# One core, a decoder layer in float32: values copied by bank, a shorter chain before the last scaling, and the weights of a compressed piece made one step later

## The chip, the cores and the metric

The kernel is one program on one core of a Trainium2 chip. The metric is the device time of one execution in microseconds (us), lower is better. Engines are named as in the profile: PE (TensorE, matmuls), PEld (its weight loads), DVE (VectorE), ACT (ScalarE), POOL (GpSimd), SP (the queue that issues most transfers).

## What is computed

The reference is one decoder layer over 256 tokens of width 2048. Two attention groups run side by side on one normed input, latent attention (MLA, 8 heads) and sparse attention (NSA, 16 heads), and their outputs are joined, projected, and followed by a squared-ReLU MLP and a last RMS norm. Cut to what the change touches:

```python
# values of MLA
kv = (rmsnorm(c_kv, kv_norm_w) @ w_ukv).reshape(B, T, MLA_HEADS, MLA_NOPE + MLA_V)
k_nope, v = kv[..., :MLA_NOPE], kv[..., MLA_NOPE:]
# NSA: keys and values compressed over blocks of 32 tokens, stride 16
blk = t[:, tok_idx] + pos[None, None, :, None, :]
k_cmp = gelu(blk @ w1) @ w2
# one head's three branches; the compressed one has 15 keys
p_c = masked_softmax(s, dist >= 0);  o_c = p_c @ v_cmp
return g0 * o_c + g1 * o_s + g2 * o_w
# end of the layer
return rmsnorm(h + square(relu(n @ w_up)) @ w_down, final_norm_w)
```

With 256 tokens every block is selected, so the selected and the window branch both see all earlier tokens.

## The kernel before, in words

Every engine has its own instruction list, written out by hand, and they meet through semaphores alone. Float32 products are made from two parts: ACT copies a weight chunk to a high part (`w_hi`, L587, L594), DVE subtracts to get the low part (`w_lo`, L885), and PE multiplies high by high, high by low and low by high. Weight chunks are numbered in the order of use.

The attention stage is a table of steps, `STEPS`: eight MLA steps, then for each pair of NSA heads five steps, `slc` and `win` of the first head, `slc` and `win` of the second, and `cmp` for both. Each engine runs `slot(i)` for i = 0, 1, 2, ..., with products of the output projection (`("q", ...)`, L1387 to L1391) and weight splits between the slots, in the order of the list `PLAN`. `LAG` is 4. In slot i

- PE makes the scores of step i (L1617, L1618 for `slc`, which also serves the `win` step after it), transposes the finished weights of step i-4 (L1635; L1630 for a `cmp` step), and multiplies those of step i-5 by the values (L1662, L1663; L1649 for `cmp`);
- DVE adds the bias to the scores of step i and takes the extreme (`masked`, L1034), and scales the exponentials of step i-2 (`weights`, L1061 to L1065; those of `slc` and `win` together);
- ACT copies PE's transposes out (L694; L692 for `cmp`) and then makes the exponentials of step i-1 (L717, L718).

The scores of the compressed branch are made for four heads at a time, in four pieces. `PIECES` maps slots 12, 22, 32 and 42 to pieces 0 to 3. In such a slot PE makes the piece's scores (L1584) and DVE takes them in (`piece_in`, L1024 to L1028); ACT makes its exponentials one slot later (L724). DVE's `piece_weights` (L1041 to L1047 and one L885 on `pcs`) turns them into weights and raises `pc_ok`, for which PE waits before it transposes the `cmp` step at L1630, four slots after the piece's scores:

```python
if kind == "cmp":
    pe.wait_ge(pc_ok, h // 4 + 1)
```

Two other places matter. The value product of MLA (chunk 20) leaves tokens 0 to 127 in PSUM banks 4 and 5; DVE copies both to `v_sb` (L1011) and raises `v_out`. The first layer of the compression (chunks 21, 23 for keys in bank 4, chunks 25, 27 for values in bank 5; L1708, L1709) waits for that before its first chunk. At the end, `root(t, ...)` (L1315) makes one over the root mean square of the tokens of half t: ACT sums the last squares (L836, `fsq`) and takes a square root (L848, `sqrt_ok`), DVE meanwhile prepares minus half the mean square (L1318, L1319) for one Newton step on the reciprocal (L1321 to L1323). `link` makes the next DVE instruction wait for the one that it wraps.

Of the kernel before, what the change touches and what calls it, by code (L numbers as in the profile page):

```python
# [61 lines left out]
def split_slot(c):  # L62
    return (c + 1) % SPLIT
# [79 lines left out]
def build(nc, a, out):  # L143
    with ExitStack() as ctx:
# [729 lines left out]
        def _(dve):  # L874
            chain = [0]

            def link(ins):
                chain[0] += 1
                ins.then_inc(dve_c, 1)
                dve.wait_ge(dve_c, chain[0])  # L880
# [127 lines left out]
            low(blk[:, :, :, 32:32 + 2 * NC].rearrange("p y k n -> p (y k) n"), blkf[:, :, :, :].rearrange("p y k n -> p (y k) n"),  # L1008
                blk[:, :, :, 0:2 * NC].rearrange("p y k n -> p (y k) n")).then_inc(blk_ok, 1)
            dve.wait_ge(w_used, UKV_V + 1)  # L1010
            dve.tensor_copy(v_sb[:, 0, :], flat[:, 2048:3072]).then_inc(v_out, 1)  # L1011

            STEP_OF = {n: i for i, n in SOFT.items()}
            vfull = h1a[:, 0, :].rearrange("p (g d) -> p g d", g=NG)
# [52 lines left out]
            def slot(i):  # L1067
                kind, u, h, branch = STEPS[i] if i < len(STEPS) else ("cmp", 0, 0, 0)
                if kind == "mla":
                    n = SOFT[i]  # L1070
                    dve.wait_ge(score_t, n + 1)
                    if n == 0:
                        dve.wait_ge(q_lo, 4)
                    masked(n, [ps[:, 4 + i % 2, 0:P], ps[:, 4 + i % 2, P:SEEN]], mask)
                elif kind == "slc":
                    n = SOFT[i]
                    dve.wait_ge(score_t, n + 2)
                    dve.wait_ge(bias_ok, h + 1)
                    for b in range(2):
                        masked(n + b, [ps[:, 4, P * b:P * b + P], ps[:, 5, T * b:T * b + T]], (bias_even, bias_odd)[h % 2])  # L1080
                if i in PIECES:
                    piece_in(PIECES[i], 5)
                if i == SUM0:
                    mean_square(0, rm[:, :])
                if 0 <= i - 2 < len(STEPS):
                    weights(STEPS[i - 2][0], STEPS[i - 2][2], SOFT.get(i - 2))
                if i - 2 in PIECES:
                    piece_weights(PIECES[i - 2])
                j = i - LAG - 1
                if j >= 0 and LASTSTEP[STEPS[j][1]] == j:  # L1090
                    u = STEPS[j][1]
                    dve.wait_ge(y_hi, u + 1)
                    low(yT[:, u, 1, :], ysb[:, u % 2, :], yT[:, u, 0, :], wcols[:, PRM["y"] + u:PRM["y"] + u + 1]).then_inc(y_lo, 1)
# [218 lines left out]
                dve.scalar_tensor_tensor(out=o, in0=flat[:, b0 + c0:b0 + c1], scalar=r1[:, t:t + 1], in1=o,  # L1312
                                         op0=ALU.mult, op1=ALU.add).then_inc(last_in, 1)

            def root(t, part, rest, done):  # L1315

                y, w, minus, mean = rc[:, t:t + 1], rc[:, 2 + t:3 + t], root_w[:, t:t + 1], root_w[:, 2 + t:3 + t]
                link(dve.scalar_tensor_tensor(out=mean, in0=part, scalar=1.0 / D, in1=rest, op0=ALU.mult, op1=ALU.add))  # L1318
                link(dve.tensor_scalar(minus, mean, -0.5, None, ALU.mult))  # L1319
                dve.wait_ge(sqrt_ok, t + 1)  # L1320
                link(dve.reciprocal(y, rm[:, t:t + 1]))  # L1321
                link(dve.scalar_tensor_tensor(out=w, in0=y, scalar=minus, in1=y, op0=ALU.mult, op1=ALU.mult))
                dve.scalar_tensor_tensor(out=y, in0=w, scalar=1.5, in1=y, op0=ALU.add, op1=ALU.mult).then_inc(done, 1)  # L1323
# [11 lines left out]
            dve.wait_ge(fsq, 2)  # L1335
            dve.tensor_scalar(ssq[:, 12:13], ssq[:, 12:13], 1.0 / D, EPS, ALU.mult, ALU.add).then_inc(rest_ok, 1)
            dve.wait_ge(rest_ok, 1)
            dve.wait_ge(fsq, 3)
            root(0, ssq[:, 13:14], ssq[:, 12:13], root0)
            dve.wait_ge(last_t, 1)  # L1340
            last_add(1, 1024, 1536)
            dve.wait_ge(root0, 1)
# [13 lines left out]
            dve.scalar_tensor_tensor(out=ssq[:, 14:15], in0=ssq[:, 10:11], scalar=1.0 / D, in1=ssq[:, 14:15],  # L1356
                                     op0=ALU.mult, op1=ALU.add).then_inc(rest_ok, 1)
            dve.wait_ge(rest_ok, 2)
            dve.wait_ge(fsq, 6)
            root(1, ssq[:, 11:12], ssq[:, 14:15], root1)  # L1360
            dve.wait_ge(root1, 1)
            last_norm(1, 1024, 1280)
            last_norm(1, 1280, D)
# [3 lines left out]
        def _(pe):  # L1367
# [320 lines left out]
            for kind, i in PLAN:  # L1688
                if kind in "wq" and (i in A_IN if kind == "w" else i[0] in A_IN):
                    c, quarter = (i, None) if kind == "w" else i  # L1690
                    j = A_IN.index(c)
                    if j in (0, 2):
                        pe.wait_ge(kv_out, 3 + j // 2)
                    if j == 4:
                        pe.wait_ge(qs_lo, 2)
                    q_products(c, quarter)
                elif kind == "w":
                    if i == CMP[0]:
                        pe.wait_ge(blk_ok, 1)
                        pe.wait_ge(v_out, 1)  # L1700
                    y, half, s = CMP.index(i) // 2, CMP.index(i) % 2, split_slot(i)
                    o = ps[0:64, 4 + y, 0:CMP_HID]
                    for b in range(8):
                        k = 8 * half + b
                        w = slice(CMP_HID * b, CMP_HID * b + CMP_HID)
                        if b % 4 == 0:
                            split_done(i, b == 0)
                        pe.matmul(o, blk[:, y, k, :], w_hi[:, s, w], start=k == 0, stop=False)  # L1708
                        m = pe.matmul(o, blk[:, y, k, :], w_lo[:, s, w], start=False, stop=k == 15)  # L1709
                        if b == 3:  # L1710
                            m.then_inc(w_half, 1)
                    m.then_inc(w_used, 1)
                elif kind == "q":
                    c, quarter = i
                    n, j, part = (c - WO_M) // 4, (c - WO_M) % 4, (c - WO_M) // 8

                    def free(t, n=n):
                        if n:
                            pe.wait_ge(dve_free, 2 * n - 1 + t)
                        else:  # L1720
                            pe.wait_ge(q_in, 2 * t + 2)
                    if n % 2 == 0 and quarter % TT == 0:
                        pe.wait_ge(y_lo, 8 * part + 2 * j + 1 + quarter // TT)
                    stream(c, of_y, 8 * part + 2 * j, LOW, j == 0, j == 3, free, quarter)
                elif kind == "s":
                    slot(i)
                elif kind == "keys":
                    pe.wait_ge(kn_out, i + 1)
                    turn_kd(2 + i, i)
                elif i == "rotary":  # L1730
                    pe.wait_ge(kn_out, 4)
                    pe.wait_ge(qpr_ok, 2)
                    for c in range(4):
                        for t in range(TT):
                            o = T * (c % 2) + P * t
                            m = pe.transpose(ps[:, 2 + c // 2, o:o + P], qpr[:, t, P * c:P * c + P], ident[:, :])
                        if c % 2:
                            m.then_inc(qp_t, 1)
                elif i == "rotary_k":
                    pe.wait_ge(v_rest, 1)  # L1740
                    pe.wait_ge(kpe_ok, 2)
                    for t in range(TT):
                        m = pe.transpose(ps[:, 6, P * t:P * t + P], kpe[:, t, :], ident[:, :])
                    m.then_inc(qp_t, 1)
                elif i == "turn":
                    pe.wait_ge(g_ok, 1)
                    pe.wait_ge(kp_lo, 1)
                    for y in range(2):
                        for k in range(2):
                            o = 2 * NC * (2 * y + k)  # L1750
                            m = pe.transpose(ps[:, 6, o:o + 2 * NC], h1a[:, y, P * k:P * k + P], ident[0:2 * NC, 0:2 * NC])
                    m.then_inc(g_t, 1)
                elif i == "project":
                    pe.wait_ge(g_turned, 1)
                    pe.wait_ge(w2_in, 48)
                    for k in range(2):
                        pe.matmul(ps[:, 7, 0:2 * NC], w2k[:, k, :, :].rearrange("p c d -> p (c d)"), h1T[:, k, :],
                                  start=k == 0, stop=k == 1)
                    for g in range(NG):
                        for k in range(2):  # L1760
                            m = pe.matmul(ps[0:2 * NC, 7, 64 + DK * g:64 + DK * g + DK],
                                          h1V[:, 2 * k + g, :, :].rearrange("p e n -> p (e n)"), w2v[:, k, :],
                                          start=k == 0, stop=k == 1)
                    m.then_inc(k_t, 1)
                elif i == "rows":
                    pe.wait_ge(rbc_ok, 2)
                    for t in range(TT):
                        m = pe.transpose(ps[:, 7, P * t:P * t + P], rtmp[:, 0, P * t:P * t + P], ident[:, :])
                    m.then_inc(rr_t, 1)
                elif i == "norm_n":  # L1770
                    sum_over_features(1)
# [123 lines left out]
```

## Time and profile before

| what | value |
|---|---|
| device time, median of 3 runs | 1051.85 us (1051.05 to 1051.92) |
| the profiled execution, device time | 1051.07 us |
| the profiled execution, span | 1049.3 us |
| PE busy | 1036.7 us |
| DVE busy | 637.0 us |
| ACT busy | 503.4 us |
| mean granted clock of PE | 0.997 |

The device time of the profiled execution is 1.8 us over its span, which reaches from the first to the last instruction on the core. Times in rows are counted from the span's start. Busy times of PE are modelled, so single gaps are read from the starts of its instructions. The attention slots lie between about 150 and 305 us, the MLP's loop between about 330 and 1020 us.

### The profile page before, as it was taken

What the parts mean: (1) busy time and instruction counts of PE and PEld (TensorE: products, weight loads), DVE (VectorE), ACT (ScalarE), POOL (GpSimd) and SP (SyncE); (2) the same over time, 40 slices, a digit from 0 to 9 for tenths busy, and PEclk for the clock granted to TensorE, in tenths of its full rate; (3) what the DMA queues carried; (4) which work ended last, traced back from release to release, by engine and by line L of the source; (5) the groups of instructions that cost most, each with busy time, mean ns of one, the idle gap of its engine ahead of it and who ended that gap; (6) DMA issues with size and microseconds to landing.
All of it is one profiled execution on the core that took longest, in us unless ns stands there. A gap on an engine that the chain in (4) does not pass through costs nothing.

```text
span 1049.3 us, 14380 instructions
## 1 busy us (share of the span) xinstructions
PE 1036.7 (99%) x5631; PEld 896.3 (85%) x5631; DVE 637.0 (61%) x761; ACT 503.4 (48%) x630; POOL 92.5 (9%) x152
## 2 busy tenths in 40 slices
PE   8999999999999999999999999999999999999996
PEld 7889999888888888888888888888888888888885
DVE  4655976988856564565456556545554555655666
ACT  5645855977754543344334443334434433433434
POOL 2135100633200100000000000000000000000002
PEclk9999999999999999999999999999999999999998
DMA  9576672343346566566556655665566565656662
GB/s 330 181 209 199 210 242 81 142 141 97 105 130 192 162 196 188 182 195 199 185 180 195 198 180 187 195 198 183 181 197 196 182 185 196 196 177 189 198 201 80
DMA packets 89137, 190.42 MB, mean 181 GB/s; under 512 B 8758, under 2 KB 29964, under 8 KB 88716
## 3 DMA queue, kind: packets, MB, share of 16 engines
q1 hardware_dynamic: 88668, 189.41, 57.3%
q10 hardware_dynamic: 432, 0.52, 0.2%
q8 instruction: 23, 0.38, 0.1%
q14 instruction: 14, 0.11, 0.0%
HBM read 187.82 MB, written 2.10 MB: 181 GB/s over the span
## 4 chain that ended last, share of the span: by engine, by line
PE 95%; DVE 2%; ACT 1%; issue 0%; DMA 0%; DVEq 0%; ACTq 0%
PE ps L1805 23%; PE ps L1387 15%; PE ps L1388 15%; PE ps L1391 15%; PE ps L1808 12%; PE ps L1678 1%; PE ps L1679 1%; PE ps L1682 1%; PE ps L1662 1%; PE ps L1635 1%; PE ps L1460 1%; PE ps L1663 1%; PE ps L1513 1%; PE ps L1512 1%; PE ps L1511 1%
## 5 line engine op out<-in xcount | busy, mean ns | idle before, releaser
L885 DVE TENSOR_TENSOR w_lo<-raw,w_hi 128x2048 fp32r<-128x2048 f32 (+4 forms) x198 | 402.4, 2034 | 355.3 <-ACT w_hi L594 289.3
L594 ACT ACTIVATE w_hi<-raw 128x2048 fp32r<-128x2048 f32 x119 | 228.1, 1917 | 399.3 <-PE ps L1391 200.7
L1805 PE MATMUL ps<-xT,w_hi 128*128 128x512 f32 x1024 | 279.4, 394 | 0.0
L1805 PEld LDWEIGHTS ps<-xT,w_hi 128*128 128x128 f32 x1024 | 176.1, 189 | 24.2
L1808 PEld LDWEIGHTS ps<-xT,w_lo 128*128 128x128 f32 x1024 | 157.2, 189 | 21.7
L1388 PE MATMUL ps<-w_lo,hidT 128*128 128x512 f32 x448 | 174.6, 390 | 0.0
L1387 PE MATMUL ps<-w_hi,hidT 128*128 128x512 f32 x448 | 174.6, 390 | 0.0
L1808 PE MATMUL ps<-xT,w_lo 128*128 128x256 f32 x1024 | 162.9, 281 | 0.0
L1391 PE MATMUL ps<-w_hi,hidT 128*128 128x512 f32 x448 | 138.2, 390 | 0.0
L587 ACT ACTIVATE w_hi<-raw 128x1024 fp32r<-128x1024 f32 (+3 forms) x75 | 104.2, 1392 | 67.9 <-PE ps L1391 40.9
L1391 PEld LDWEIGHTS ps<-w_hi,hidT 128*128 128x128 f32 x448 | 84.1, 188 | 17.6
L1388 PEld LDWEIGHTS ps<-w_lo,hidT 128*128 128x128 f32 x448 | 84.2, 188 | 17.2
L1387 PEld LDWEIGHTS ps<-w_hi,hidT 128*128 128x128 f32 x448 | 84.1, 188 | 17.1
L556 POOL TENSOR_TENSOR h_sb<-h_sb,fw 128x1024 f32<-128x1024 f32 x2 | 6.2, 3114 | 676.5 <-ACT sink L836 676.5
L1387 PE MATMUL ps<-w_hi,yT 128*128 128x512 f32 x128 | 54.0, 422 | 0.3 <-DVE h_sb L1121 0.3
L1388 PE MATMUL ps<-w_lo,yT 128*128 128x512 f32 x128 | 50.2, 392 | 0.0
L1387 PE MATMUL ps<-w_hi,xT 128*128 128x512 f32 x112 | 39.7, 355 | 0.0
L1391 PE MATMUL ps<-w_hi,yT 128*128 128x512 f32 x128 | 39.7, 392 | 0.0
L1388 PE MATMUL ps<-w_lo,xT 128*128 128x512 f32 x112 | 37.9, 349 | 0.0
L1678 PE MATMUL ps<-xT,w_hi 128*128 128x256 f32 x128 | 36.7, 286 | 0.0
L1679 PE MATMUL ps<-xT,w_hi 128*128 128x256 f32 x128 | 36.2, 283 | 0.0
L1682 PE MATMUL ps<-xT,w_lo 128*128 128x256 f32 x128 | 36.2, 283 | 0.0
(339 smaller groups left out, 1267.5 us busy)
## 6 DMA issues: line engine op xcount, KB each, us to landing
raw<-in_w_up SPq DMA_DIRECT2D x64, 1024.0 KB, 5.3
raw<-in_w_down SPq DMA_DIRECT2D x64, 1024.0 KB, 5.5
raw<-in_w_o SPq DMA_DIRECT2D x16, 1024.0 KB, 5.5
raw<-in_w_in SPq DMA_DIRECT2D x8, 1024.0 KB, 5.3
raw<-in_w_in SPq DMA_DIRECT2D x8, 816.0 KB, 4.5
raw<-in_w_in SPq DMA_DIRECT2D x6, 832.0 KB, 9.0
raw<-in_mla_w_uq SPq DMA_DIRECT2D x12, 256.0 KB, 4.6
raw<-in_mla_w_ukv SPq DMA_DIRECT2D x4, 512.0 KB, 4.9
```

The source lines that it names most:

```text
L587: act.activation(w_hi[:, split_slot(c), w0:w1], raw[:, raw_slot(c), w0:w1], ACT.Copy)\
L594: act.activation(w_hi[:, j % SPLIT, :], raw[:, j % RAW, :], ACT.Copy).then_inc(hi_done, 1)
L885: return dve.tensor_tensor(dst, src, high.bitcast(F32), ALU.subtract)
L1387: pe.matmul(o, stationary(0, b, t), w_hi[:, slot, w], start=first, stop=False)
L1388: pe.matmul(o, stationary(0, b, t), w_lo[:, slot, w], start=False, stop=False)
L1391: m = pe.matmul(o, stationary(1, b, t), w_hi[:, slot, b * width + n0:b * width + n1], start=False, stop=last)
L1460: m = pe.matmul(flat[:, LOW[t] + n0:LOW[t] + n1], of_x(part, 2 * c + b, t), w_part[:, split_slot(c), CW * b + n0:CW * b + n1], start=c == ...
L1678: pe.matmul(o, w_hi[:, s, w], xT[:, 0, k, :], start=k == 0 and f == 0, stop=False)
L1679: m = pe.matmul(o, w_hi[:, s, w], xT[:, 1, k, :], start=False, stop=False)
L1682: m = pe.matmul(o, w_lo[:, s, w], xT[:, 0, k, :], start=False, stop=k == KT - 1 and f == 1)
L1805: pe.matmul(both, w_hi[:, slot, 512 * b + P * f:512 * b + P * f + P], xT[:, :, k0 + b, :], start=start and b == 0, stop=False)
L1808: m = pe.matmul(ps[:, b0 + f, 0:T], w_lo[:, slot, 512 * b + P * f:512 * b + P * f + P], xT[:, 0, k0 + b, :], start=False, stop=stop and b ...
```

## The change

It has three edits. The copy of the MLA values from banks 4 and 5 becomes two copies of one bank each, and each of the compression's products waits only for its own bank. In the last chain, DVE's two small operations before the reciprocal are put another way, so that one of them needs only what is there before the last sum of squares. And DVE calls `piece_weights` in slot i for the piece of slot i-3, where it was i-2. PE's list of instructions stays as it is.

```diff
             dve.wait_ge(w_used, UKV_V + 1)
-            dve.tensor_copy(v_sb[:, 0, :], flat[:, 2048:3072]).then_inc(v_out, 1)
+            for n in range(2):
+                dve.tensor_copy(v_sb[:, 0, 512 * n:512 * n + 512], bank(4 + n)).then_inc(v_out, 1)
...
                 if 0 <= i - 2 < len(STEPS):
                     weights(STEPS[i - 2][0], STEPS[i - 2][2], SOFT.get(i - 2))
-                if i - 2 in PIECES:
-                    piece_weights(PIECES[i - 2])
+                if i - 3 in PIECES:
+                    piece_weights(PIECES[i - 3])
...
-            def root(t, part, rest, done):
+            def root(t, part, rest, before, done):
 
-                y, w, minus, mean = rc[:, t:t + 1], rc[:, 2 + t:3 + t], root_w[:, t:t + 1], root_w[:, 2 + t:3 + t]
-                link(dve.scalar_tensor_tensor(out=mean, in0=part, scalar=1.0 / D, in1=rest, op0=ALU.mult, op1=ALU.add))
-                link(dve.tensor_scalar(minus, mean, -0.5, None, ALU.mult))
+                y, w, minus, half = rc[:, t:t + 1], rc[:, 2 + t:3 + t], root_w[:, t:t + 1], root_w[:, 2 + t:3 + t]
+                link(dve.tensor_scalar(half, rest, -0.5, None, ALU.mult))
+                dve.wait_ge(fsq, before)
+                link(dve.scalar_tensor_tensor(out=minus, in0=part, scalar=-0.5 / D, in1=half, op0=ALU.mult, op1=ALU.add))
                 dve.wait_ge(sqrt_ok, t + 1)
                 link(dve.reciprocal(y, rm[:, t:t + 1]))
...
             dve.wait_ge(rest_ok, 1)
-            dve.wait_ge(fsq, 3)
-            root(0, ssq[:, 13:14], ssq[:, 12:13], root0)
+            root(0, ssq[:, 13:14], ssq[:, 12:13], 3, root0)
...
             dve.wait_ge(rest_ok, 2)
-            dve.wait_ge(fsq, 6)
-            root(1, ssq[:, 11:12], ssq[:, 14:15], root1)
+            root(1, ssq[:, 11:12], ssq[:, 14:15], 6, root1)
...
                     if i == CMP[0]:
                         pe.wait_ge(blk_ok, 1)
-                        pe.wait_ge(v_out, 1)
                     y, half, s = CMP.index(i) // 2, CMP.index(i) % 2, split_slot(i)
+                    pe.wait_ge(v_out, y + 1)
```

The third edit moves instructions on DVE. This is DVE's list before, from slot 34 (the third piece, scored in slot 32) into slot 35: a weight split, the piece's six instructions, and then the first of slot 35's biased scores. The rest of those scores and then the scaling of step 33 (L1061 to L1065) follow.

```order
L885 TENSOR_TENSOR w_lo<-raw,w_hi 128x1024
L1041 TENSOR_REDUCE cden<-pc 128x8
L1042 RECIPROCAL cden<-cden 128x8
L1043 TENSOR_TENSOR cden<-cden,cgate 128x8
L1044 TENSOR_TENSOR pc<-pc,cden 128x120
L1047 CAST pcs<-pc 128x4x2x30
L885 TENSOR_TENSOR pcs<-pc,pcs 128x4x30
L1034 ISA prob,nmax<-ps,bias_odd 128x128
L1034 ISA nmax 128x1
```

This is the end of slot 35 on DVE in the changed kernel (its lines are numbered one higher from L1012 on): the last of the biased scores, the scaling of step 33, and now the piece's six instructions.

```order
L1035 ISA nmax 128x1
L1062 RECIPROCAL scl<-den 128x4
L1063 TENSOR_TENSOR scl<-scl,gates 128x4
L1065 TENSOR_TENSOR prob<-prob,scl 128x2x128
L1066 TENSOR_TENSOR prob<-prob,scl 128x2x256
L1042 TENSOR_REDUCE cden<-pc 128x8
L1043 RECIPROCAL cden<-cden 128x8
L1044 TENSOR_TENSOR cden<-cden,cgate 128x8
L1045 TENSOR_TENSOR pc<-pc,cden 128x120
L1048 CAST pcs<-pc 128x4x2x30
L885 TENSOR_TENSOR pcs<-pc,pcs 128x4x30
L885 TENSOR_TENSOR w_lo<-raw,w_hi 128x1024
```

The six instructions moved from ahead of slot 35's eight score instructions and four scaling instructions to behind them. At the other three pieces the same six move past the same twelve; at piece 0 also past the two low parts of the queries (`q2b`), and at pieces 1 and 3 past a weight split.

This is DVE's second `root` before, from the sum that it starts with to the reciprocal.

```order
L1356 SCALAR_TENSOR_TENSOR ssq<-ssq 128x1
L1318 SCALAR_TENSOR_TENSOR root_w<-ssq 128x1
L1319 TENSOR_SCALAR root_w<-root_w 128x1
L1321 RECIPROCAL rc<-rm 128x1
L1322 SCALAR_TENSOR_TENSOR rc<-rc,root_w 128x1
```

And this is the same place in the changed kernel.

```order
L1357 SCALAR_TENSOR_TENSOR ssq<-ssq 128x1
L1319 TENSOR_SCALAR root_w<-ssq 128x1
L1321 SCALAR_TENSOR_TENSOR root_w<-ssq,root_w 128x1
L1323 RECIPROCAL rc<-rm 128x1
L1324 SCALAR_TENSOR_TENSOR rc<-rc,root_w 128x1
```

The count is the same; the wait for the last sum of squares stood ahead of the first of the two `root_w` operations and now stands between them.

## Rows read from the trace of the kernel before

**Rows 1.** The page: busy time of each engine

```profile
PE 1036.7 (99%) x5631; PEld 896.3 (85%) x5631; DVE 637.0 (61%) x761; ACT 503.4 (48%) x630; POOL 92.5 (9%) x152
```

**Rows 2.** Stretches: PE, PEld, DVE, ACT, POOL busy (count), clock, DMA share, GB/s

```profile
320.00:1020.00 700.00, 700.00 (x3565) 596.41 (x3564) 391.88 (x240) 282.15 (x194) 3.52 (x1) 1.00 0.61 190
```

**Rows 3.** PE's waits after 100 us: us in total, times, longest

```profile
PE ps L1635 <- DVE prob L1065: 0.6, 1, 0.6
```

**Rows 4.** Timeline of DVE around piece 2: start, us, instruction

```profile
259.29 0.27 DVE L1041 TENSOR_REDUCE cden<-pc 128x8 f32<-128x120 f32 x1
...
260.67 0.28 DVE L885 TENSOR_TENSOR pcs<-pc,pcs 128x120 fp32r<-128x120 f32 x1
260.87 0.28 DVE L1034 CUSTOM_DVE_ANT_0 prob<-ps,bias_odd 128x128 f32<-128x128 f32 x1
...
261.98 0.17 DVE L1061 RECIPROCAL scl<-den 128x4 f32<-128x4 f32 x1
...
263.33 1.22 DVE L885 TENSOR_TENSOR w_lo<-raw,w_hi 128x1024 fp32r<-128x1024 f32 x1
```

**Rows 5.** Timeline of PE, slots 35 and 36

```profile
259.88 0.40 PE L1618 MATMUL ps<-k2l,q2b 128*128 128x512 f32 x1
...
262.49 0.38 PE L1630 MATMUL ps<-ident,pcs 128*96 128x128 f32 x2
```

**Rows 6.** Timeline around piece 0, and the next `q2b` pair

```profile
206.07 1.27 ACT L771 ACTIVATE q2b<-qfb 64x512 fp32r<-64x512 f32 x2
...
208.87 0.38 PE L1630 MATMUL ps<-ident,pcs 128*96 128x128 f32 x2
...
219.13 1.27 ACT L771 ACTIVATE q2b<-qfb 64x512 fp32r<-64x512 f32 x2
...
221.26 0.29 DVE L1034 CUSTOM_DVE_ANT_0 prob<-ps,bias_odd 128x128 f32<-128x128 f32 x1
```

**Rows 7.** Timeline of DVE and PE around piece 1

```profile
233.20 0.26 DVE L1041 TENSOR_REDUCE cden<-pc 128x8 f32<-128x120 f32 x1
...
234.77 1.22 DVE L885 TENSOR_TENSOR w_lo<-raw,w_hi 128x1024 fp32r<-128x1024 f32 x1
...
237.77 0.69 DVE L1065 TENSOR_TENSOR prob<-prob,scl 128x512 f32<-128x512 f32 x1
...
235.58 0.38 PE L1630 MATMUL ps<-ident,pcs 128*96 128x128 f32 x2
...
237.40 0.62 PE L1391 MATMUL ps<-w_hi,yT 128*128 128x512 f32 x2
238.60 0.52 PE L1635 MATMUL ps<-ident,prob 128*128 128x128 f32 x3 [0.58 <-DVE prob L1065]
```

**Rows 8.** Timeline of DVE and PE around the values' copy

```profile
115.05 1.22 DVE L1011 COPY v_sb<-ps 128x1024 f32<-128x1024 f32 x1
...
117.31 0.69 DVE L885 TENSOR_TENSOR k2l<-ps,k2h 128x512 fp32r<-128x512 f32 x1
...
115.13 1.04 PE L1736 MATMUL ps<-ident,qpr 128*128 128x128 f32 x8
116.37 0.30 PE L1708 MATMUL ps<-w_hi,blk 128*64 128x256 f32 x1 [0.20 <-issue]
...
118.29 0.28 PE L1678 MATMUL ps<-xT,w_hi 128*128 128x256 f32 x1
```

**Rows 9.** Timeline of the last chain, tokens 128 to 255

```profile
1042.93 0.29 ACT L848 ACTIVATE rm<-ssq 128x1 f32<-128x1 f32 x1
...
1043.38 0.16 DVE L1321 RECIPROCAL rc<-rm 128x1 f32<-128x1 f32 x1
```

**Rows 10.** PE's last matmul, and stretches behind it (columns as in rows 2)

```profile
1041.07 0.28 PE L1858 MATMUL ps<-w_end,hidZ 128*128 128x256 f32 x1
...
1043.00:1044.00 1.00, 0.00 (x0) 0.00 (x0) 0.85 (x5) 0.22 (x1) 0.00 (x0) 1.00 1.03 422
1044.00:1044.50 0.50, 0.00 (x0) 0.00 (x0) 0.47 (x2) 0.47 (x1) 0.00 (x0) 0.50 0.43 164
```

## Prediction, made before the result was known

> **What bounds the kernel now.** I read the page's first part first: PE is busy for 1036.7 of 1049.3 us and no other engine comes near [rows 1]. Then the stretches: in the MLP's 700 us PE is busy for all 700 at full clock [rows 2]. So a microsecond that PE loses in the attention stage isn't won back later. It moves everything behind it, and the end. Then PE's own waits after 100 us: the longest is 0.6 us, for the scaled probabilities of DVE at L1065 [rows 3]. The kernel is bound by PE's stream, with DVE close behind it in the attention slots. There the question for any edit on DVE is when a result is ready and when PE comes for it, so I went to the timelines of both engines at the three places that the change touches.
>
> **The piece's weights, one slot later.** PE's list doesn't move: it still comes for `pc_ok` in the fourth slot after the piece's scores. What moves is DVE's part, from ahead of the next slot's twelve instructions to behind them. Those twelve can't be done before PE has made that slot's scores. This gives a floor that can be worked out from four durations, all at piece 2:
>
> - The six instructions of the piece run from 259.29 to 260.67 + 0.28 = 260.95, so 1.66 us [rows 4].
> - Slot 35's biased scores run from 260.87 to 261.98, 1.11 us, and the scaling from there to 263.33, 1.35 us [rows 4].
> - PE's scores of slot 35 end at 259.88 + 0.40 = 260.28, and PE comes for the piece at 262.49 [rows 5]. That is 2.21 us.
> - A hand-over from DVE to PE takes 0.14 us: L1065 ends at 237.77 + 0.69 = 238.46 and PE's L1635, which waited for it, starts at 238.60 [rows 7].
>
> Before, the piece was ready 1.54 us ahead of PE (262.49 - 260.95). Now DVE needs 1.11 + 1.35 + 1.66 + 0.14 = 4.26 us after the scores are there, and PE leaves it 2.21. PE stalls for 2.05 us; with a hand-over of up to 0.14 from PE to DVE as well, 2.19. I take **2.1**. DVE's earlier start doesn't help, since the scores hold it: without the piece it would be free at 259.29 and the scores end at 260.28. The exponentials that the scaling needs are no later than before. Piece 3 has the same distance between the same two PE rows and the same twelve instructions; the weight split that is moved past there too finds room ahead of the scores. So the rows of piece 2 stand for both: 2 x 2.1 = **4.2**.
>
> At piece 1 DVE runs behind PE, with no idle time in these rows. Between 233.20 and 238.46 it does the piece, a weight split (234.77), the biased scores, and the scaling that ends with L1065 [rows 7]. The same instructions in another order end at the same time, 238.46, now with the piece's last one. PE comes for it at 235.58 and would go on at 238.60: a stall of **3.0**. In return the wait for L1065 at 238.60 goes, 0.58 by its row, since the scaling is now 1.6 us earlier and PE is later: **-0.6**. The floor here is the 2.1 of piece 2, were DVE not behind.
>
> At piece 0 the `q2b` pair stands behind the piece too. It can't start early, since it waits for ACT's pair of copies, started at 206.07. At the next such place DVE idles for ACT, and slot 20's biased scores start 221.26 - 219.13 = 2.13 us after ACT's pair [rows 6]. So here they start at 206.07 + 2.13 = 208.20. Then 1.11 + 1.35 + 1.66 + 0.14 gives 212.46, and PE comes at 208.87 [rows 6]: a stall of **3.6**. That second `q2b` place also matters because DVE there falls in step with ACT, and ACT with PE's transposes. The lead over PE that DVE wins in the first stall is gone before piece 1.
>
> Together 3.6 + 3.0 - 0.6 + 4.2 = 10.2 us. ACT is held in each stall too, as its list has the copy of PE's transpose (L692) ahead of the exponentials. They then come as much later as PE does, and the next use of each is two slots off, so I charge nothing for that. If that cover were gone, another wait of up to the same length would follow.
>
> **The clock.** The last matmul ends at 1041.07 + 0.28 = 1041.35. The granted clock is still 1.00 (2.4 GHz) in the stretch to 1044.00 and 0.50 (1.2 GHz) from there [rows 10]. So it held for 2.65 us of idleness and then fell. Stalls of 2.1 us are shorter than that, those of 3.0 and 3.6 longer. Were it to fall, no row shows how long it stays down once PE works again. I bound that by the time that it took to fall: 2.65 us at half speed lose 1.3 us, so 0 to 1.3 for each of the two long stalls. In the sum I take 0, as one observation with nothing behind it, no matmul at all, is not a stall inside a dense stream.
> The Trainium skill, "TensorE: Matmul & The Clock Gate", Part 1, has the low clock as the default that activity lifts, and its section on oscillation has a stream that waits for operands falling back at its breaks. The trace agrees that the clock falls after idleness. By that rule alone the sum would be up to 2.7 us higher, and by the row's 2.65 us it stays where it is for two of the four stalls at least.
>
> **The values by bank.** L1708 starts at 116.37, 0.10 after the copy of both banks ends at 115.05 + 1.22 = 116.27 [rows 8]. PE's eight transposes before it end at 116.17 by their row, so the wait costs at least 0.20, as the row says, and at most 0.4, if L1708 could follow the transposes at their own pace (1.04 us for eight with the overlap of the last, so some 0.11 each: 115.13 + 8 x 0.11 = 116.0). The first half copy is done by some 0.7 after 115.05 (a 128x512 on DVE takes 0.69), so this wait goes. What is late next is `k2l`: PE needs it for its next product at 118.29, and it ends at 117.31 + 0.69 = 118.00 at the earliest, a little later with the second copy's overhead [rows 8]. With the hand-over of 0.14 the product can't start before 118.14. Gain 0 to 0.4; I take **-0.1**.
>
> **The last chain.** The square root ends at 1042.93 + 0.29 = 1043.22 and the reciprocal starts at 1043.38, behind the two small operations [rows 9]. One of them now lies in DVE's wait for the sum of squares. The reciprocal still needs the root, so at most 0.16 is to be had, and nothing at the least; **-0.1**. The first `root` has the root as its last input already and lies beside PE's work: 0.
>
> **Sum.** 10.2 - 0.1 - 0.1 = +10.0 us. The profiled execution took 1051.07 us (span 1049.3), which gives 1061.1. It lies 0.8 below the median of the runs shown, 1051.85, from which it would be 1061.9. I forecast between them, **1061.4 us**.
>
> **Rivals.**
>
> - *Four stalls, clock held* (my forecast), 0.50: 1061.4, its own range 1060.3 to 1062.4.
> - *The clock falls in one or both of the long stalls*, 0.28: +1.3 or +2.7, so 1062.7 to 1064.1. For it speaks that 3.0 and 3.6 exceed 2.65 us; against it, that PE is dense on both sides. The page named above is this rule.
> - *DVE gets ahead for good*, 0.15. If the lead after the first stall lasts, or ACT's pair at piece 0 comes sooner, every stall shrinks toward the floor: 4 x 2.1 - 0.6 - 0.2 = +7.6, 1059.0. Against it speaks DVE's idle time for ACT ahead of 221.26.
> - *Faster*, 0.04. One mechanism, the wait at L1635: if the piece were ready when PE comes, only the gains would be left, 0.6 + 0.1 + 0.1, so 1050.6. It decides at 2.21 us between scores and transposes: DVE would have to do 4.26 us of work in them, or PE to come 2.1 us later than its rows say. Nothing in the rows shows such slack.
> - *No change by measure*, 0.03: the stalls are taken up by waits that PE has anyway. Rows 3 name the longest as 0.6, so there is too little to take up. That the edit doesn't reach the instructions is excluded by their order.
>
> A measurement tells about 0.2% here, 2.1 us. Slower by more: 0.50 + 0.28 + 0.15 = 0.93. Within: 0.03. Faster: 0.04. The range runs from the third case's 1059.0, a little below, to the second's 1064.1, a little above: 1058.8 to 1064.2.
>
> **What would show it.** In the changed profile PE idles ahead of L1630 four times, for about 3.6, 3.0, 2.1 and 2.1 us, released by DVE's L885 on `pcs`, and ACT's wait for L692 grows by the same. PE's wait at L1635 for L1065 is gone. L1708 starts some 0.3 us earlier after its transposes, L1678 about 0.1. The reciprocal of the second `root` starts less than 0.16 after the square root's end. The granted clock between 205 and 245 us tells the second case. I am wrong if DVE does the piece before slot i's scores in time, or if PE's L1630 starts within 0.5 us of where its stream reaches it.

## The result and the profile after

The changed kernel takes 1067.19 us (median of 4 runs, 1065.64 to 1067.36), the kernel before 1051.82. The ratio is 1.0145, 95% interval 1.0132 to 1.0157: 15.4 us slower. The direction was forecast, the size was not: 1067.2 lies above the range's 1064.2.

The profiled execution took 1067.03 us with a span of 1065.2, 15.9 more than before. The first two lines of its page answer to [rows 1]: PE has the same 5631 instructions and 6.5 us more of busy time, which no added work explains.

```profile
span 1065.2 us, 14384 instructions
...
PE 1043.2 (98%) x5631; PEld 900.4 (85%) x5631; DVE 636.8 (60%) x762; ACT 503.5 (47%) x630; POOL 93.3 (9%) x152
```

PE's waits in the attention slots (in total, times, longest). The wait of [rows 3] is gone, and the one that was forecast is there four times:

```profile
PE ps L1630 <- DVE pcs L885: 10.1, 4, 3.4
PE ps L1387 <- DVE h_sb L1122: 0.3, 1, 0.3
```

The four places on PE's timeline: the last product before the wait, then the first transpose of the piece, with PE's idle time in brackets.

```profile
208.38 0.62 PE L1391 MATMUL ps<-w_hi,yT 128*128 128x512 f32 x2
212.40 0.63 PE L1630 MATMUL ps<-ident,pcs 128*96 128x128 f32 x2 [3.40 <-DVE pcs L885]
...
241.34 0.61 PE L1391 MATMUL ps<-w_hi,yT 128*128 128x512 f32 x2
244.80 0.40 PE L1630 MATMUL ps<-ident,pcs 128*96 128x128 f32 x2 [2.85 <-DVE pcs L885]
...
272.06 0.63 PE L1391 MATMUL ps<-w_hi,yT 128*128 128x512 f32 x2
274.64 0.40 PE L1630 MATMUL ps<-ident,pcs 128*96 128x128 f32 x2 [1.94 <-DVE pcs L885]
...
300.32 0.63 PE L1391 MATMUL ps<-w_hi,yT 128*128 128x512 f32 x2
302.89 0.40 PE L1630 MATMUL ps<-ident,pcs 128*96 128x128 f32 x2 [1.94 <-DVE pcs L885]
```

From the first of L1391's two products to L1630 a stream without a wait takes about 0.46 us (235.12 to 235.58 in the kernel before). The stalls are the rest: 4.02 - 0.46 = 3.56, then 3.00, 2.12 and 2.11 us, each as forecast. The times in brackets are up to 0.2 us shorter; below, "idle" means the bracket and "stall" the loss by the starts. DVE at the third of them, as the floor in the prediction had it: the biased scores wait for PE's scores, then 1.12 us of them, 1.35 of scaling, and 1.67 for the piece, which ends 0.15 before L1630 starts.

```profile
270.35 0.29 DVE L1035 CUSTOM_DVE_ANT_0 prob<-ps,bias_odd 128x128 f32<-128x128 f32 x1 [0.94 <-PE ps L1618]
...
271.47 0.17 DVE L1062 RECIPROCAL scl<-den 128x4 f32<-128x4 f32 x1
...
272.82 0.27 DVE L1042 TENSOR_REDUCE cden<-pc 128x8 f32<-128x120 f32 x1
...
274.21 0.28 DVE L885 TENSOR_TENSOR pcs<-pc,pcs 128x120 fp32r<-128x120 f32 x1
```

So the stalls are 10.8 us. The wait that went was worth 0.74 by the starts (L1391 at 237.40 to L1635 at 238.60 is 1.20 in the kernel before, where 0.46 is the pace), which leaves 10.05. The span grew by 15.9. The rest is in the stretches (length, busy time of PE, PEld, DVE, ACT, POOL, then granted clock, DMA share, GB/s):

```profile
208.00:211.20 3.20, 1.00 (x5) 0.47 (x3) 3.03 (x16) 0.91 (x1) 0.00 (x0) 1.00 0.97 324
211.40:218.00 6.60, 5.60 (x20) 4.86 (x20) 2.30 (x7) 3.07 (x10) 0.00 (x0) 0.50 0.43 171
218.20:244.80 26.60, 23.75 (x133) 19.81 (x131) 22.40 (x69) 16.77 (x46) 9.88 (x19) 1.00 0.25 80
245.40:248.60 3.20, 3.20 (x11) 2.42 (x10) 1.52 (x5) 1.96 (x9) 0.00 (x0) 0.50 0.52 127
248.80:303.40 54.60, 50.72 (x284) 42.84 (x283) 40.40 (x129) 35.23 (x100) 13.65 (x11) 1.00 0.27 88
303.60:306.80 3.20, 3.20 (x10) 2.42 (x10) 1.53 (x5) 1.85 (x9) 0.00 (x0) 0.50 0.51 146
```

The granted clock is at 0.50 (1.2 GHz) in three stretches, each of which begins in a stall or within 0.6 us of its end, and lasts about 6.8, 3.4 and 3.4 us. I call such a change from 1.00 to 0.50 a fall. What that does to the matmuls is seen in the spacing of the products behind the fourth stall, 0.43 us in place of 0.24:

```profile
304.56 0.63 PE L1388 MATMUL ps<-w_lo,yT 128*128 128x512 f32 x1
304.99 0.63 PE L1387 MATMUL ps<-w_hi,yT 128*128 128x512 f32 x1
...
307.00 0.36 PE L1649 MATMUL ps<-probR,vcmp 96*128 96x256 f32 x1
307.20 0.40 PE L1387 MATMUL ps<-w_hi,yT 128*128 128x512 f32 x1
307.44 0.40 PE L1388 MATMUL ps<-w_lo,yT 128*128 128x512 f32 x1
```

From L1630 to L1649 it is 307.00 - 302.89 = 4.11 us here and 291.11 - 288.61 = 2.50 in the kernel before: 1.6 us for one stretch of 3.4. Behind the second stall it is 4.11 too (3.30 in the kernel before, with the wait for L1065 in it, and 2.52 in an execution of the changed kernel whose clock held there), behind the first 5.51 where it was 2.90, so 1.6 and 2.6. Together 5.8 us, and 10.05 + 5.8 = 15.9.

### The profile page after: what moved, and what is told of

It reads as the page before. It is cut to its first block, busy times and chain, and to the rows that moved or that the text cites. A ratio compares the mean times of both kernels' runs of the same rounds, so it can differ in the third digit from the quotient of the medians.

```text
span 1065.2 us, 14384 instructions
## 1 busy us (share of the span) xinstructions
PE 1043.2 (98%) x5631; PEld 900.4 (85%) x5631; DVE 636.8 (60%) x762; ACT 503.5 (47%) x630; POOL 93.3 (9%) x152
## 4 chain that ended last, share of the span: by engine, by line
PE 93%; DVE 4%; ACT 2%; issue 1%; DMA 0%; DVEq 0%; ACTq 0%
PE ps L1805 22%; PE ps L1387 15%; PE ps L1388 15%; PE ps L1391 15%; PE ps L1808 11%; PE ps L1678 1%; PE ps L1679 1%; PE ps L1682 1%; PE ps L1662 1%; PE ps L1460 1%; PE ps L1635 1%; DVE prob L1035 1%; PE ps L1663 1%; PE ps L1513 1%; PE ps L1511 1%
## 5 line engine op out<-in xcount | busy, mean ns | idle before, releaser
L1805 PE MATMUL ps<-xT,w_hi 128*128 128x512 f32 x1024 | 279.3, 394 | 0.0
L1805 PEld LDWEIGHTS ps<-xT,w_hi 128*128 128x128 f32 x1024 | 176.0, 189 | 24.3
L1388 PE MATMUL ps<-w_lo,hidT 128*128 128x512 f32 x448 | 174.4, 389 | 0.0
L1391 PE MATMUL ps<-w_hi,hidT 128*128 128x512 f32 x448 | 138.1, 389 | 0.0
L1391 PEld LDWEIGHTS ps<-w_hi,hidT 128*128 128x128 f32 x448 | 84.1, 188 | 17.6
L1388 PEld LDWEIGHTS ps<-w_lo,hidT 128*128 128x128 f32 x448 | 84.1, 188 | 17.2
L1387 PE MATMUL ps<-w_hi,yT 128*128 128x512 f32 x128 | 55.6, 434 | 0.3 <-DVE h_sb L1122 0.3
L1388 PE MATMUL ps<-w_lo,yT 128*128 128x512 f32 x128 | 51.6, 403 | 0.0
L1391 PE MATMUL ps<-w_hi,yT 128*128 128x512 f32 x128 | 41.0, 403 | 0.0
L1388 PE MATMUL ps<-w_lo,xT 128*128 128x512 f32 x112 | 37.9, 348 | 0.0
L1678 PE MATMUL ps<-xT,w_hi 128*128 128x256 f32 x128 | 36.7, 287 | 0.1
```

The costliest lines, as they stand in the source:

```text
L1387: pe.matmul(o, stationary(0, b, t), w_hi[:, slot, w], start=first, stop=False)
L1388: pe.matmul(o, stationary(0, b, t), w_lo[:, slot, w], start=False, stop=False)
L1391: m = pe.matmul(o, stationary(1, b, t), w_hi[:, slot, b * width + n0:b * width + n1], start=False, stop=last)
L1678: pe.matmul(o, w_hi[:, s, w], xT[:, 0, k, :], start=k == 0 and f == 0, stop=False)
L1805: pe.matmul(both, w_hi[:, slot, 512 * b + P * f:512 * b + P * f + P], xT[:, :, k0 + b, :], start=start and b == 0, stop=False)
```

## The experiments

One measure is used for all. Executions differ in how long their first 85 us take: PE's first product of chunk 16 (L1523) starts between 84.87 and 86.62 us in the profiled ones, and between 85.11 and 86.03 in the four of the changed kernel. So beside the times I give the **way**: from that product to the MLP's first matmul (L1805), in the profiled execution. It is 331.66 - 85.11 = 246.55 us before and 347.56 - 85.11 = 262.45 in the changed kernel: +15.9, the whole difference of the spans. Four executions of one kernel further down have ways from 248.60 to 248.66, so a few hundredths of a microsecond are noise. The way ends before the last chain, of which it says nothing.

### Which edit it is

The first kernel puts the pieces' weights back, the second makes that edit alone.

```diff
-                if i - 3 in PIECES:
-                    piece_weights(PIECES[i - 3])
+                if i - 2 in PIECES:
+                    piece_weights(PIECES[i - 2])
```

> The changed kernel with the piece's weights made in slot i-2 again, so that only the copy by bank and the shorter chain are left. Theory: the two edits are worth 0.1 us together, PE never waits at L1630 and the clock stays at 1.00, so -0.1 us against the kernel before (1051.7). Rival: one of the two small edits carries part of the loss of 15.4 us; then this is over 1053.

> The kernel before with only the piece's weights moved to slot i-3. Theory: all of the loss is here, +15.5 us (between +13.8 and +17, by how many of the stalls end with the clock at 1.2 GHz). Rival: the edits work on each other, and this alone loses clearly less.

Measured: 1051.62 us with the pieces back, ratio 1.0003 (0.9993 to 1.0012), way 246.50. With the pieces alone 1067.66 us, ratio 1.0153 (1.0136 to 1.0170), way 262.48. All of the loss is in this edit. The copy by bank is worth 0.05 us of way at most, no more than the noise of the way, and neither small edit shows in the times.

### The stalls without the clock

The rival to "stalls and a lower clock" was that a stall brings further waits behind it. Here PE is kept at work during the stalls, on transposes whose output nothing uses.

```diff
+                        if j in PIECES:
+                            for _ in range((30, 24, 17, 17)[PIECES[j]]):
+                                pe.transpose(ps[:, 6, SEEN:SEEN + P], ident[:, :], ident[:, :])
                         pe.wait_ge(pc_ok, h // 4 + 1)
```

> The changed kernel, in which PE makes 30, 24, 17 and 17 transposes of the identity into an unused part of bank 6 ahead of its four waits for the piece's weights (some 0.11 us each, so 3.2, 2.6, 1.8 and 1.8 us, less than the stalls of 3.6, 3.0, 2.1 and 2.1). Nothing else is changed and their output is not used. Theory (stalls of 10.1 us in all, and 5.8 us from the clock falling during them): the clock stays at 1.00 and the time is +10.0 us against the kernel before. Rival (the 5.8 us are knock-on waits or contention after a stall, and the clock's level follows something else): still +15.4 us.

Measured: 1060.83 us, ratio 1.0091 (1.0074 to 1.0108), +9.3 us. All four runs lie between 1060.65 and 1060.91. The way is 256.34, +9.8. The clock stays at 1.00, and PE comes to the first piece's transposes 127.2 us after the product at 85 us (212.06 - 84.87), where it was 127.3 with an idle stall (212.40 - 85.11):

```profile
205.00:335.00 130.00, 129.48 (x732) 109.89 (x731) 91.83 (x251) 79.87 (x207) 25.98 (x32) 1.00 0.38 124
```

```profile
208.56 3.44 PE L1630 MATMUL ps<-ident 128*128 128x128 f32 x30
212.06 0.42 PE L1633 MATMUL ps<-ident,pcs 128*96 128x128 f32 x2
```

PE has more work, and the way is 6.1 us shorter than the changed kernel's (by the times 15.4 - 9.3 = 6.1 too). This parts the loss: 9.8 us of way are the stalls, and 6.1 went with the idleness. Most of the 6.1 is the clock. The four stalls are 0.06 to 0.10 us shorter each than the idle ones (3.96 for 4.02 from L1391 to the piece's transposes at the first), 0.3 together, so 5.8 is left for the clock, which is what the rows above gave.

### Half of each stall filled

The same with 15, 12, 8 and 8 transposes.

> As the kernel with the stalls filled, with half as many transposes (15, 12, 8 and 8), so that PE still idles for about 2.0, 1.7, 1.2 and 1.2 us in each stall. The stalls' 10 us stay in any case. If the clock falls by the length of idle time alone and 1.9 us is near the least that does it (it fell at one of the two stalls of that length in the changed kernel), at most one fall is left: +10 to +11.6 us. If any stall of this kind can bring it down, two or three falls: +13 to +15.

Measured: 1060.79 us (1060.48 to 1061.42), ratio 1.0087 (1.0070 to 1.0104), way 256.23. PE still idles for 5.1 us in four waits (1.68, 1.43, 0.98 and 0.98), and the clock is at 1.00 throughout the attention slots. The first outcome came, with no fall at all. The mean granted clock was 0.998 in all four runs, and so it was in the four with the stalls filled:

```profile
209.42 1.80 PE L1630 MATMUL ps<-ident 128*128 128x128 f32 x15
...
212.90 0.42 PE L1633 MATMUL ps<-ident,pcs 128*96 128x128 f32 x2 [1.68 <-DVE pcs L885]
```

### One piece late at a time

The edit for piece 0; those for pieces 2 and 3 differ only in the numbers.

```diff
-                if i - 3 in PIECES:
-                    piece_weights(PIECES[i - 3])
+                for back, those in ((2, (1, 2, 3)), (3, (0,))):
+                    if PIECES.get(i - back) in those:
+                        piece_weights(PIECES[i - back])
```

> The changed kernel with only piece 0 one slot later, the others in slot i-2. Theory: one stall of 3.6 us and 2.6 us of PE work at 1.2 GHz behind it (1.6 if the low clock lasts as it did at pieces 1 and 3), so +6.1 or +5.1 us; the stall at piece 1 for L1065 is as before. Rival: the lead that DVE wins stays, and the wait for L1065 at piece 1 shrinks, so 0.7 less.

> The changed kernel with only piece 2 one slot later. Theory: a stall of 2.1 us at PE and nothing else, +2.0 us; if the clock falls in it as it did at piece 3 of the changed kernel, +3.6 us. Rival: a stall of 2.1 us is taken up elsewhere, under +1.

> The changed kernel with only piece 3 one slot later. Same stall of 2.1 us: +2.0 us with the clock held, +3.6 us with a fall. If falls come by chance with the moment, runs of this kernel and of the one with piece 2 late lie on two levels 1.6 us apart; if the place decides, piece 3 is always +3.6 and piece 2 always +2.0.

Measured with piece 0 late: 1057.18 us, ratio 1.0057 (1.0040 to 1.0073), way 251.59, +5.0. PE's idle time at the piece is 3.43 us, the clock is at 0.50 for 3.4 us from 0.2 us before its end, and the wait for L1065's result at piece 1 is 0.6 us as before. So DVE's lead is lost by then, and the third rival of the prediction is out.

With piece 2 late: 1054.67 us, ratio 1.0028 (1.0017 to 1.0038), way 248.66, +2.1, clock held. With piece 3 late: 1054.68 us, ratio 1.0030 (1.0020 to 1.0040), way 248.60, +2.05, clock held. The ways and the clock are those of the profiled executions. A stall of 2.1 us goes to the end in full.

Each median is a microsecond more than the way of the profiled execution tells. The mean granted clock, which is measured in every run, says why for the most part. A fall of 3.4 us takes 1.7 us of clock off some 1054, 0.0016 of the mean. It was 0.997 to 0.999 in every run of the kernel before, and 0.996 in the two profiled executions with one fall of 3.4 us (piece 0 late, and the piece between, below). The nine runs of piece 3 are these:

| mean granted clock | times, us |
|---|---|
| 0.998 or 0.999 | 1053.23, 1053.40 (profiled), 1053.61, 1054.15, 1054.68 |
| 0.996 | 1055.83, 1056.03, 1056.03, 1056.12 |

So four of the nine had a fall, at the same stall in the same kernel. Of the eight runs of piece 2, four were at 0.996 too (1054.68 to 1055.17), one at 0.997, which tells neither, and three at 0.998 or 0.999 (1054.03 to 1054.65); there the two groups lie less than 1.6 us apart. The runs without a fall have medians of 1053.61 and 1054.31, +1.95 and +2.65 against the kernel before.

> The same kernel as with only piece 3 late, profiled again. Its nine times lay near 1053.4 and near 1056. If falls come by the moment and not by the place, the profile shows one stall of 1.9 to 2.0 us in every execution and the clock at 0.50 behind it in some of them, with 1.6 us more from L1630 to the MLP's first matmul in these.

> The same kernel once more, same expectation: the stall always, the fall in some executions, 1.6 us apart.

> The same kernel once more, same expectation: the stall always, the fall in some executions, 1.6 us apart.

These gave 1053.45, 1054.10 and 1053.52 us, ways of 248.66, 248.65 and 248.63, and no fall in any. The mean clock was 0.998 in each. The expectation of falls in some was not met by these three; it had been met by the nine before them.

### The same kernel again

> The changed kernel unchanged, profiled again. The four stalls at L1630 are the same as before in length to 0.1 us (3.6, 3.0, 2.1, 2.1). If the falls of the clock come by the moment, their number and length differ between executions, and the way from the first product of chunk 17 (85 us) to the MLP's first matmul differs with them: 246.5 + 10.0 us, plus 1.6 us for each fall of one period (3.4 us) at 1.2 GHz. If the place decides: three falls, at pieces 0, 1 and 3, and 262.4 us each time.

> The changed kernel once more, same expectation as for the first repeat: stalls the same, 246.5 + 10.0 us of way plus 1.6 us per 3.4 us at 1.2 GHz; by the moment, the number differs; by the place, 262.4 us again.

> The changed kernel once more, same expectation as for the first repeat: stalls the same, 246.5 + 10.0 us of way plus 1.6 us per 3.4 us at 1.2 GHz; by the moment, the number differs; by the place, 262.4 us again.

(The product at 85 us is the first of chunk 16.) The times were 1064.35, 1066.78 and 1067.91 us, the ways 259.46, 262.21 and 262.42. PE's wait at L1630 is 10.1, 10.1 and 10.2 us. The stretches at 0.50, in the first,

```profile
212.20:215.40 3.20, 2.68 (x9) 2.33 (x10) 1.47 (x3) 2.01 (x9) 0.00 (x0) 0.50 0.80 321
...
300.80:304.00 3.20, 3.20 (x10) 2.46 (x9) 1.53 (x5) 2.00 (x9) 0.00 (x0) 0.50 0.49 120
```

and in the second:

```profile
211.00:217.60 6.60, 5.18 (x17) 4.44 (x18) 2.29 (x7) 3.07 (x10) 0.00 (x0) 0.50 0.48 182
245.20:248.40 3.20, 3.20 (x10) 2.55 (x9) 1.52 (x5) 2.01 (x9) 0.00 (x0) 0.50 0.50 124
275.80:279.00 3.20, 3.20 (x11) 2.59 (x10) 1.37 (x4) 2.75 (x9) 0.00 (x0) 0.50 0.00 0
```

The first has falls at pieces 0 and 3, the second at 0, 1 and 2, the third at 0, 1 and 3, with 6.8 us at piece 1 and not at piece 0. The same stalls bring different falls: it is the moment, not the place. Nor has PE to be idle when the clock changes. At piece 2 of the second, L1630 starts at 274.46 and the stretch at 0.50 only 1.3 us later:

```profile
274.46 0.40 PE L1630 MATMUL ps<-ident,pcs 128*96 128x128 f32 x2 [1.94 <-DVE pcs L885]
...
275.83 0.63 PE L1387 MATMUL ps<-w_hi,yT 128*128 128x512 f32 x1
276.26 0.63 PE L1388 MATMUL ps<-w_lo,yT 128*128 128x512 f32 x1
```
In the first, with two stretches of 3.4 us, the way is 3.1 us longer than with the stalls filled, about 1.6 for each, as expected.

### Where DVE's order is the hold-up, and where it isn't

Two more tested the floor's arithmetic and the wait of [rows 3]. In one, slot i makes the weights of slot i-3's piece between its biased scores and its scaling, ahead of the scaling and not behind it; in the other the pieces are back and one weight split of DVE moves behind slot 25.

```diff
+                if i - 3 in PIECES:
+                    piece_weights(PIECES[i - 3])
                 if 0 <= i - 2 < len(STEPS):
                     weights(STEPS[i - 2][0], STEPS[i - 2][2], SOFT.get(i - 2))
-                if i - 3 in PIECES:
-                    piece_weights(PIECES[i - 3])
```

```diff
+LATE_SPLIT = NMLA + 17
...
-        behind = [i for i in split if i[0] == "lo" and _s in PIECES]
+        behind = [i for i in split if i[0] == "lo" and (_s in PIECES or _s == LATE_SPLIT)]
```

> The changed kernel with the piece's weights in slot i-3 between the biased scores and the scaling, 1.35 us sooner than behind the scaling. By the floor's arithmetic the stalls become 2.2, 1.7, 0.75 and 0.75 us, less 0.7 for the wait at L1065: +4.6 us with the clock held, +6.2 with one fall at piece 0. Rival (the hold-up isn't DVE's order after the scores): stalls as in the changed kernel, +10 or more.

> The piece's weights in slot i-2, the two small edits kept, and the weight split that stands ahead of slot 25 on DVE (first half of chunk 38) put behind that slot, 1.1 us of work out of the way of the scaling of step 23, for which PE waited 0.7 us at L1635. Theory: that wait goes, -0.8 us against the kernel before. Rival: the half split is then late for PE, or the wait moves to the next scaling: 0 or more.

Measured with the piece between: 1057.73 us, ratio 1.0051 (1.0034 to 1.0068), way 252.74, +6.2. PE idles for 2.05, 1.49, 0.59 and 0.59 us at the four pieces, 1.35 less than in the changed kernel each time, and the clock falls once, at piece 0. Both terms are as expected. One of the four runs took 1055.51 us at a mean clock of 0.998, where the other three have 0.996 and 1057.57 to 1058.43, so by that figure the clock held there once at the same stall.

With the split behind slot 25: 1051.36 us, ratio 0.9995 (0.9986 to 1.0005), way 246.10, -0.45. The wait at L1635 is gone, but the gain is about half of the 0.8 that was expected, and too little for the times to tell from nothing, so this isn't shown to beat the kernel before. Some of the 0.7 us comes back behind the next matmul, where PE loses 0.18 us (0.38 us from L1650 to L1388, 0.20 elsewhere).

## Why the prediction was wrong

- **What bounds it**: right. PE's stalls in the attention slots reached the end in full: +9.8 us with all four and the clock held, +2.1 and +2.05 with one of the short ones.
- **The four stalls**: right. 3.6, 3.0, 2.1 and 2.1 were forecast and measured, the wait for L1065 went, and with the stalls filled the way is +9.8 for the 10.0 of the sum. The wait that went was worth 0.74, not the 0.58 of its row. That DVE's order after the scores is the cause is shown by the kernel with the piece in between.
- **The step that failed is the clock**: "In the sum I take 0", with 0 to 1.3 us for each of two stalls as its bound. It measured 5.8 us in the profiled execution. Two things were off. I let the stalls of 2.1 us go free because the clock had held for 2.65 us behind PE's last matmul [rows 10]; but it fell at one of the two here, at an idle time of 1.94 us. One sample of how long the clock held was read as the least that it always holds. And the price of a fall was put at half of 2.65; the low level lasted 3.4 or 6.8 us, worth 1.6 to 2.6. With four falls at 1.6 the range would have reached 1061.4 + 6.4 = 1067.8, above all four runs. "Not a stall inside a dense stream" was no reason: PE was dense on both sides and the clock fell.
- The rule of the Trainium skill that was weighed there ("TensorE: Matmul & The Clock Gate", its section on oscillation), that a stream which waits for operands falls back at its breaks, had the direction right. The trace agrees, with three falls at four breaks, and it should have weighed more than the one row.
- **The rivals**: the clock's fall was the right one, at 0.28, but priced only up to 1064.1. DVE's lasting lead did not come (the wait at piece 1 was unchanged with piece 0 late).
- **The values by bank**: L1708 starts 0.47 us earlier (115.90 for 116.37), L1678 only 0.18 earlier (118.11 for 118.29), and with the pieces back 0.05 us of way is left. Forecast 0.1.
- **The last chain**: wrong, by a little. The reciprocal starts 0.10 us after the square root's end, where it was 0.16, so the sign that was named came. But the square root starts later itself. Counted from PE's last matmul the reciprocal starts 1059.32 - 1056.97 = 2.35 us on, and 1043.38 - 1041.07 = 2.31 in the kernel before. It is 2.34 or 2.35 in every profiled execution with this edit and 2.31 in the two without it (the kernel before, and the pieces alone). Forecast a gain of 0.1, measured a loss of 0.03 to 0.04. In the new order the sum of squares of L1357 starts 1.70 us after the last matmul, where L1356 started 1.37 after it; why is open.

```profile
1056.97 0.28 PE L1858 MATMUL ps<-w_end,hidZ 128*128 128x256 f32 x1
...
1058.67 0.16 DVE L1357 SCALAR_TENSOR_TENSOR ssq<-ssq 128x1 f32<-128x1 f32 x1 [0.36 <-DVE ssq L1354]
...
1059.32 0.16 DVE L1323 RECIPROCAL rc<-rm 128x1 f32<-128x1 f32 x1
```

## What to carry to other kernels

When a result is made later on one engine, take the stretch between the last input that this engine waits for and the moment when the consumer comes, and add up what now has to be done in it: here 4.26 us in 2.21 at the third and fourth piece, and worse at the first two, where DVE was behind or held by ACT. When the consumer is the matmul engine at full clock, price each stall twice, once as itself and once for a fall of the clock, and let the upper bound hold a fall for every stall of about two microseconds or more. Where PE has to wait anyway, matmuls of no use kept the clock up, also when they filled only half of the wait, and took about 6 us off the changed kernel; not to have the wait is 9.3 us better still. Two more things carry over. The mean granted clock of a run that wasn't profiled can tell whether it had a fall. And a sign such as "the reciprocal starts sooner after the square root" is worth nothing until it is counted from a landmark that the edit can't move.

## What the runs showed of the hardware

Counted over the profiled executions of all kernels here, by PE's idle time at the wait: the clock fell at 6 of 6 stalls of 3.4 us, at 4 of 5 of 2.8, at the one of 2.05, at 5 of 15 of 1.94, and at none of 7 between 0.6 and 1.7. The mean clocks of the runs with one piece late point the same way for 1.94 us: four of nine and four of eight had a fall. Each time the low level lasted about 3.4 or 6.8 us, also with PE busy all the while. The fall came as early as 1.5 us before PE's next matmul and as late as 1.4 us after its start. That a busy engine stays at half speed for 3.4 us or more after idling for 1.9 was new to me. What decides between a fall and none at the same stall is not settled beyond that it changes from one execution to the next; the changed kernel's times, from 1064.4 to 1067.9 us, go with it.
